# Rotary partners of queries and keys by a partition shuffle, with their squares on ScalarE

## The chip, the cores and the metric

One of the cores of a Trainium2 chip runs the whole program. The metric is the device time of one execution in microseconds. Five engines matter: TensorE (PE; its weight loads are PEld), VectorE (DVE), ScalarE (ACT), GpSimd (POOL) and SyncE (SP), which issues the loads of weights.

## What is computed

Two layers of a hybrid block (a convolution, a retention and a window attention branch on one input projection), and then one layer of another block. Sequence 512, width 1024, all in fp32. The change touches the attention branch of the two hybrid layers alone:

```python
def window_attention_branch(q, k, v, gate, q_norm_g, k_norm_g, sink, positions):
    q = rms_norm(q.reshape(B, S, ATTN_HEADS, HEAD_DIM), q_norm_g)      # 16 heads of 64
    k = rms_norm(k.reshape(B, S, ATTN_KV_HEADS, HEAD_DIM), k_norm_g)   # 4 heads of 64
    q = rotary(q, positions, ROPE_THETA, ROPE_DIM)                     # first 16 of each 64
    k = rotary(k, positions, ROPE_THETA, ROPE_DIM)
    ...
    s = jnp.where(valid, s, -1e30)                                     # window of 128 to each side
    m = jnp.maximum(jnp.max(s, axis=-1, keepdims=True), sink_l)
    p = jnp.exp(s - m)
    p = p / (jnp.sum(p, axis=-1, keepdims=True) + jnp.exp(sink_l - m))
    o = jnp.einsum('bhgnqj,bnjhd->bnqhgd', p, vwin)
    return o.reshape(B, S, ATTN_HEADS * HEAD_DIM) * jax.nn.silu(gate)

def rotary(x, positions, theta, rot_dim):
    x1, x2 = x[..., :half], x[..., half:rot_dim]                       # half is 8
    return concatenate([x1 * cos - x2 * sin, x2 * cos + x1 * sin, x[..., rot_dim:]])
```

## The kernel before

Activations lie transposed: a tile is 128 features (partitions) by 512 positions. A weight slab is 128x1024. SyncE loads it into one of two `raw` buffers; ScalarE rounds it to fp32r (`high`, L832, tile `whi`), GpSimd takes the rest (`low`, L275, `wlo`), each into one of four buffers. TensorE then makes each product as three fp32r matmuls, high by high, high by low, low by high (L330 to L332 in `gemm`, L521 to L523 in `rows`). Results stand in the four banks of `gem`; a bank is free when `evac` of it has counted up. The other PSUM tensor, `xp`, has four banks for everything that is not a slab product. Every engine has its program written out by hand, in order; they meet only at semaphores.

Keys and queries of the attention branch are ten tiles of two heads each, `NORMED[0..9]`: two of keys, eight of queries. For each tile n:
- VectorE squares it into the scratch `RT[0]` (`square`, L1600, signal `a_sq`)
- TensorE adds the squares over each 64 partitions: a product with the block matrix `blk64` into bank 0 of `xp` (`a_norm`, L484, signal `a_ssq`). This and the next are plain fp32 matmuls, which the chip runs as two passes
- ScalarE makes the inverse root by logarithm and exponential into `RS` (`a_inv`, L849 and L851, signal `a_rs`)
- VectorE multiplies by it (`a_normed`, L1606, signal `a_kn`)
- TensorE multiplies by a rotation matrix `rot` into bank 1 of `xp` (`a_turn`, L489, signal `a_rot`)
- VectorE rotates: tile times cosines into `RT[1]` (L1612), `xp` times sines into `RT[2]` (L1614), sum (L1616, signal `a_rope`). This is `a_rotated`

Tiles 0 to 5 go through this while TensorE makes the queries' first half and the last retention head's output product (`half`; its results are added to `yr` on VectorE, L1555). "The head" below is that stretch. Tiles 6 to 9 go through it in the attention stage: TensorE first makes slabs 0 to 3 (queries' second half, `rows(k, ...)`) and then goes through 24 steps t, three per pair of heads (p = t // 3). In step t it makes the scores of step t (`qk`, L544; from step 2 on it waits for `p_exp` of step t - 2's exponentials), transposes the probabilities of step t - 3 (`turn_p`, L562), multiplies step t - 4's with the values (`a_pv`, L578), and makes a part of gate slab 4 + p (`rows`) in between. ScalarE makes the exponentials of a step (`exps`, L1027), copies transposed probabilities to `PT`, and a tanh for the gate (L1047); VectorE makes the masked maxima (`maxes`, L1660 to L1666), the normaliser (`normalise`, L1673 and L1675, for the first step of a pair L1683 too) and the gate (L1689, which frees bank 3). GpSimd scales the probabilities of the other two steps (L284).

The scratch lies where other buffers live later: `RT[0]` and `RT[1]` in the first buffer of transposed probabilities `PT[0]`, `RT[2]` in the second, `PT[1]`. So the transposes of step 0 wait for all ten rotations (`a_rope`).

Of the kernel before, what the change touches and what calls it, by code (L numbers as in the profile page):

```python
# [26 lines left out]
PAD = TAPS // 2  # L27

# [41 lines left out]
def build(nc, ins, out, xsave):  # L70
# [5 lines left out]
    with ctx:  # L76
# [17 lines left out]
        rot = sb("rot", [P, P])  # L94
# [37 lines left out]
        RT = [U[:, a:a + T] for a in (U_C + 2 * T, U_C + 3 * T, U_SG + 2 * T)]  # L132
# [41 lines left out]
        def sem(name):  # L174
# [32 lines left out]
        a_sq, a_ssq, a_rs, a_kn, a_rot, a_rope = (sem(n) for n in (  # L207
            "a_sq", "a_ssq", "a_rs", "a_kn", "a_rot", "a_rope"))
# [105 lines left out]
        def _(pe):  # L314
# [70 lines left out]
            def layer(L):  # L385
# [6 lines left out]
                if L == 0:  # L392
                    pe.wait_ge(const_in, 16 * 6)
# [105 lines left out]
                for k in range(1, 4):  # L499
                    hslab(G + 2, k, u + 2)  # L500
                    if k > 1:
                        a_turn(k - 2)
                    a_norm(k - 1)
                for k in range(4):
                    half(G + 3, k, u + 3, (z_ready, L * 40 + 12 + PRIMED) if k == 0 else None)
                    a_turn(k + 2)
# [41 lines left out]
                def turn_p(t):  # L548
# [6 lines left out]
                    if t == 0:  # L555
                        pe.wait_ge(a_rope, L * 10 + 10)
# [27 lines left out]
                for k in range(1, 4):  # L584
# [3 lines left out]
                    a_turn(k + 5)  # L588
                    if k == 2:
                        qk(0)  # L590
                for t in range(1, 24):
# [7 lines left out]
                    if t == 2:  # L599
                        a_turn(9)  # L600
# [216 lines left out]
        def _(act):  # L817
# [4 lines left out]
            for n, (dst, name) in enumerate(((ident, "ident"), (blk64, "blk64"), (rot, "rot"), (amask, "amask"),  # L822
# [65 lines left out]
            def layer(L):  # L888
# [101 lines left out]
                read(0, QR[0], A.Copy)  # L990
                for v in range(2):
# [4 lines left out]
                for k in range(1, 4):  # L996
                    tick(G + 2, k)
                    read(k, QR[k], A.Copy)
                    a_inv(k - 1)
                high(G + 3, 3)  # L1000
                for k in range(3):
                    high(G + 3, k + 4)
                    a_inv(k + 3)

                act.wait_ge(z_ready, L * 40 + 16 + PRIMED)
                G, u = g0 + ATT[0], u0 + ATT[1]
                tick(G, 0)
                read(0, QR[4], A.Copy)

# [21 lines left out]
                for k in range(1, 4):  # L1031
# [5 lines left out]
                    read(k, QR[4 + k], A.Copy)  # L1037
                for t in range(1, 27):
# [294 lines left out]
        def _(dve):  # L1333
# [84 lines left out]
            def layer(L):  # L1418
# [29 lines left out]
                if L == 0:  # L1448
                    dve.wait_ge(const_in, 16 * 6)
# [142 lines left out]
                ua = u0 + ATT[1]  # L1592

                def square(n):
                    dve.drain()
                    if n >= 6:
# [648 lines left out]
```

## Time and profile before

| | |
|---|---|
| Median of 3 runs | 3121.58 us (3121.37 to 3121.99) |
| The profiled execution | 3118.49 us |
| Its span, first to last instruction | 3116.7 us |
| Mean granted TensorE clock | 0.995 of full |
| Busy: PE, DVE, ACT, POOL | 98%, 55%, 35%, 45% of the span |

A busy share is an average over very different stages. In a row of the timeline stand start, duration, engine, line, operation, the tiles written and read, and in brackets how long the engine had been idle and who ended that. Matmuls are pipelined: their durations overlap, and the step from one start to the next is what one costs.

### The profile page before, as it was taken

How to read it: one execution, taken by the hardware profiler on the slowest of the kernel's cores; microseconds unless marked ns; L12 is line 12 of the kernel's file. 1: busy time of each engine (PE TensorE's matmuls, PEld its weight loads, DVE VectorE, ACT ScalarE, POOL GpSimd, SP SyncE). 2: the span in 40 equal slices, each digit the busy share in tenths (PEclk: the TensorE clock that was granted, in tenths of full speed). 3: DMA queues.
4: the chain of work that ended last, by engine and by line, in shares of the span. 5: the costliest groups of instructions: out<-in, count | busy, mean ns of one | idle time of the engine just before them, and what ended most of it. 6: DMA issues, size and time to landing. Idle time of an engine off the chain costs nothing.

```text
span 3116.7 us, 40813 instructions
## 1 busy us (share of the span) xinstructions
PE 3050.8 (98%) x13780; PEld 2404.0 (77%) x13780; DVE 1706.2 (55%) x2577; ACT 1092.9 (35%) x1635; POOL 1398.9 (45%) x1030
## 2 busy tenths in 40 slices
PE   7999999999999999999999999999999999999997
PEld 5877777767888787777776788877888887788886
DVE  7974575675434597576566644267763253621214
ACT  3232332354332223233235524235554332422223
POOL 4433543445555443443344455443334444454443
PEclk9999999999999999999999999999999999999999
DMA  3221222212222321221221132221212322222222
GB/s 139 95 73 69 94 71 78 81 42 82 95 101 98 112 103 68 95 74 67 81 82 54 35 129 95 100 88 61 71 70 88 103 86 97 85 102 95 96 100 81
DMA packets 73408, 267.86 MB, mean 86 GB/s; under 512 B 8144, under 2 KB 9168, under 8 KB 72912
## 3 DMA queue, kind: packets, MB, share of 16 engines
q1 hardware_dynamic: 70560, 254.84, 23.6%
q10 hardware_dynamic: 2736, 11.53, 1.0%
q8 instruction: 70, 1.15, 0.1%
q14 instruction: 42, 0.34, 0.0%
HBM read 262.14 MB, written 4.19 MB: 85 GB/s over the span
## 4 chain that ended last, share of the span: by engine, by line
PE 83%; issue 7%; POOL 5%; DVE 3%; DVEq 1%; ACT 1%; ACTq 0%; POOLq 0%
PE gem L330 18%; PE gem L332 18%; PE gem L331 18%; POOL wlo L275 5%; PE xp L434 4%; PE gem L410 2%; PE gem L409 2%; PE gem L411 2%; PE xp L423 2%; PE gem L521 2%; PE gem L523 1%; PE gem L522 1%; PE gem L544 1%; PE xp L578 1%; PE gem L677 1%
## 5 line engine op out<-in xcount | busy, mean ns | idle before, releaser
L275 POOL TENSOR_TENSOR wlo<-raw,whi 128x512 fp32r<-128x512 f32 x956 | 1318.9, 1401 | 1641.3 <-ACT whi L832 1640.5
L330 PE MATMUL gem<-hhi,whi 128*128 128x512 f32 x2032 | 813.0, 400 | 0.0
L332 PE MATMUL gem<-hhi,wlo 128*128 128x512 f32 x2032 | 791.3, 389 | 0.0
L331 PE MATMUL gem<-hlo,whi 128*128 128x512 f32 x2032 | 790.7, 389 | 0.0
L832 ACT ACTIVATE whi<-raw 128x1024 fp32r<-128x1024 f32 x478 | 504.4, 1056 | 679.7 <-PE gem L332 488.6
L330 PEld LDWEIGHTS gem<-hhi,whi 128*128 128x128 f32 x2032 | 381.6, 188 | 90.3 <-issue 12.9
L331 PEld LDWEIGHTS gem<-hlo,whi 128*128 128x128 f32 x2032 | 381.7, 188 | 89.7 <-issue 12.2
L332 PEld LDWEIGHTS gem<-hhi,wlo 128*128 128x128 f32 x2032 | 381.4, 188 | 79.8
L330 PE MATMUL gem<-zhi,whi 128*128 128x512 f32 x960 | 378.6, 394 | 2.9 <-DVE zlo L1346 2.9
L332 PE MATMUL gem<-zhi,wlo 128*128 128x512 f32 x960 | 374.1, 390 | 0.0
L331 PE MATMUL gem<-zlo,whi 128*128 128x512 f32 x960 | 374.0, 390 | 0.0
L841 ACT ACTIVATE U<-gem 128x512 f32<-128x512 f32 x150 | 89.2, 597 | 507.6 <-PE gem L332 456.0
L330 PEld LDWEIGHTS gem<-zhi,whi 128*128 128x128 f32 x960 | 180.4, 188 | 43.2 <-DVE zlo L1346 3.5
L331 PEld LDWEIGHTS gem<-zlo,whi 128*128 128x128 f32 x960 | 180.5, 188 | 39.6 <-issue 2.4
L332 PEld LDWEIGHTS gem<-zhi,wlo 128*128 128x128 f32 x960 | 180.4, 188 | 37.8
L1474 DVE SCALAR_TENSOR_TENSOR xp<-cv,sm,xp 128x512 f32<-128x512 f32 x224 | 159.1, 752 | 17.2 <-issue 15.0
L1441 DVE SCALAR_TENSOR_TENSOR xp<-cv,vec,xp 128x512 f32<-128x512 f32 x224 | 159.0, 752 | 9.2
L841 ACT ACTIVATE U<-gem,vec 128x512 f32<-128x512 f32 x96 | 65.5, 684 | 252.8 <-PE gem L332 217.7
L2055 DVE TENSOR_TENSOR U<-gem,U 128x512 f32<-128x512 f32 x22 | 15.2, 691 | 185.5 <-PE gem L332 185.5
L1346 DVE TENSOR_TENSOR zlo<-U,zhi 128x512 f32 (+1 forms) x88 | 107.8, 1225 | 11.4 <-issue 0.8
L434 PE MATMUL xp<-U 128*128 128x512 f32 x256 | 112.5, 592 | 0.0
L677 PE MATMUL gem<-hhi,whi 128*128 128x512 f32 x256 | 107.4, 419 | 0.5 <-POOL wlo L275 0.5
(265 smaller groups left out, 3902.1 us busy)
## 6 DMA issues: line engine op xcount, KB each, us to landing
raw<-in_slabs SPq DMA_DIRECT2D x478, 512.0 KB, 3.2
U<-in_x SPq DMA_DIRECT2D x4, 512.0 KB, 7.5
U<-in_x ACTq DMA_DIRECT2D x1, 2048.0 KB, 8.2
xsave<-U ACTq DMA_DIRECT2D x1, 2048.0 KB, 6.3
U<-xsave ACTq DMA_DIRECT2D x1, 2048.0 KB, 8.3
out_y<-yr SPq DMA_DIRECT2D x8, 256.0 KB, 2.1
tab<-in_tab_ret ACTq DMA_DIRECT2D x2, 512.0 KB, 8.0
tab<-in_tab_att ACTq DMA_DIRECT2D x2, 512.0 KB, 3.6
```

The source lines that it names most:

```text
L275: part = pool.tensor_tensor(wlo[:, k % 4, c], raw[:, k % 2, c], whi[:, k % 4, c].bitcast(f32), O.subtract)
L330: pe.matmul(o, wh, hi, start=(n == 0), stop=False)
L331: pe.matmul(o, wh, lo, start=False, stop=False)
L332: mm = pe.matmul(o, wl, hi, start=False, stop=(n == len(terms) - 1))
L409: pe.matmul(o, hhi[:, k, c], wh, start=(k == 0), stop=False)
L434: mm = pe.matmul(xp[:, v % 2, :], VT[:, j, v * P:(v + 1) * P], ST[:, j, :], start=(j == 0), stop=(j == 3))
L677: pe.matmul(gem[:, k, :], wh, hhi[:, r, :], start=(r == 0), stop=False)
L832: act.activation(whi[:, k % 4, :], raw[:, k % 2, :], A.Copy).then_inc(hi_done, 1)
L841: act.activation(dst, gem[:, b, :], func, bias=bias, scale=scale).then_inc(evac[b], 1)
L1346: tt(lo, src, hi.bitcast(f32), O.subtract).then_inc(count, 1)
L1441: stt(acc if n < TAPS - 1 else TT[:, 0, :], v, w, acc, O.mult, O.add)
L1474: stt(acc if n < TAPS - 1 else TT[:, 0, :], v, w, acc, O.mult, O.add)
```

## The change

It computes the rotated partner on VectorE. A shuffle of the 32 partitions of each quadrant swaps rows 0 to 7 with rows 8 to 15 (`PARTNER`), and the sign that was in the matrix `rot` is now in the sine table. `rot`, its load, `a_turn` and the signal `a_rot` are gone. The squares are activations on ScalarE, right after it has read a tile's bank or, for tiles that are there already, after the inverse root of the tile before. `RT[1]` and `RT[2]` both lie in the second buffer `PT[1]`; so the transposes of step 0 wait only for the tenth inverse root, those of step 1 for the ten rotations, and the last rotation is made in step 3 instead of step 2. VectorE normalises step 0 ahead of the maxima of step 1 and makes a head tile's rotation ahead of the addition to `yr`.

```diff
+PARTNER = [r + 8 if r < 8 else r - 8 if r < 16 else r for r in range(32)]
...
-        RT = [U[:, a:a + T] for a in (U_C + 2 * T, U_C + 3 * T, U_SG + 2 * T)]
+        RT = [U[:, a:a + T] for a in (U_C + 2 * T, U_SG + 2 * T, U_SG + 3 * T)]
...
# TensorE
-                def a_turn(n):
-
-                    pe.wait_ge(a_kn, L * 10 + n + 1)
-                    pe.matmul(xp[:, 1, :], rot[:, :], NORMED[n], start=True, stop=True).then_inc(a_rot, 1)
...
                     if t == 0:
+                        pe.wait_ge(a_rs, L * 10 + 10)
+                    elif t == 1:
                         pe.wait_ge(a_rope, L * 10 + 10)
...
# ScalarE
                 def a_inv(n):
                     act.wait_ge(a_ssq, L * 10 + n + 1)
+                    if n:
+                        act.wait_ge(a_kn, L * 10 + n)
                     inv_sqrt(RS, xp[:, 0, :], 64, EPS, a_rs)
+
+                def a_square(n):
+
+                    act.activation(RT[0], NORMED[n], A.Square).then_inc(a_sq, 1)
...
                 read(0, QR[4], A.Copy)
+                act.drain()
+                a_square(6)
...
                     read(k, QR[4 + k], A.Copy)
+                    act.drain()
+                    a_square(k + 6)
...
# VectorE
                     tt(RT[1], x, tab[:, 0, :], O.mult)
-                    dve.wait_ge(a_rot, L * 10 + n + 1)
-                    tt(RT[2], xp[:, 1, :], tab[:, 1, :], O.mult)
+                    dve.stream_shuffle(RT[2], x, PARTNER)
+                    dve.drain()
+                    tt(RT[2], RT[2], tab[:, 1, :], O.mult)
...
                 maxes(0)
                 a_rotated(7)
                 a_normed(8)
-                square(9)
+                normalise(0)
+                maxes(1)
                 a_rotated(8)
-                maxes(1)
-                normalise(0)
                 a_normed(9)
                 for t in range(2, 24):
                     p, c = t // 3, t % 3
                     maxes(t)
                     normalise(t - 1)
-                    if t == 2:
+                    if t == 3:
                         a_rotated(9)
...
# tables
-            cos[h + r:h + r + 8], sin[h + r:h + r + 8] = ca, sa
+            cos[h + r:h + r + 8], sin[h + r:h + r + 8] = ca, sa if r else -sa
```

On TensorE, in the head, after the second slab of queries, this piece of the difference (a minus is a row of before that is gone) stands six times per layer, with small variations:

```order
 L331 MATMUL gem<-hlo,whi 128x512
 L332 MATMUL gem<-hhi,wlo 128x512
-L489 MATMUL xp<-U,rot 128x512
 L484 MATMUL xp<-U,blk 128x512
 L330 MATMUL gem<-hhi,whi 128x512
```

The rotation between the slab and the sum over squares is gone; the slab's last matmul and the sum now follow each other.

On ScalarE, at attention slabs 0 and 1, before (`U<-gem` is the read of a bank, `whi<-raw` the conversion of a weight slab, the two rows with `U` after it an inverse root):

```order
L841 ACTIVATE U<-gem 128x512
L832 ACTIVATE whi<-raw 128x1024
L849 ACTIVATE U<-xp,sm 128x512
L851 ACTIVATE U<-U 128x512
L841 ACTIVATE U<-gem 128x512
L832 ACTIVATE whi<-raw 128x1024
```

and in the change (L984 is the square):

```order
L832 ACTIVATE U<-gem 128x512
L984 ACTIVATE U<-U 128x512
L823 ACTIVATE whi<-raw 128x1024
L840 ACTIVATE U<-xp,sm 128x512
L842 ACTIVATE U<-U 128x512
L832 ACTIVATE U<-gem 128x512
L984 ACTIVATE U<-U 128x512
```

A square now stands between the read of a tile and the next weight conversion.

On VectorE, in step 2 of the attention stage, before: the end of the maxima, the normaliser of step 1, the last rotation (L1612, L1614, L1616), the gate, and the maxima of step 3.

```order
L1664 SCALAR_TENSOR_TENSOR sm<-sm 128x2
L1666 TENSOR_TENSOR sm<-sm 128x2
L1673 TENSOR_TENSOR sm<-sm 128x2
L1675 RECIPROCAL sm<-sm 128x2
L1612 TENSOR_TENSOR U<-U,tab 128x512
L1614 TENSOR_TENSOR U<-xp,tab 128x512
L1616 TENSOR_TENSOR U<-U 128x512
L1689 SCALAR_TENSOR_TENSOR U<-U,gem 128x512
L1660 ISA gem,sm<-gem,amask 128x256
```

In the change, in step 3: the end of the maxima of step 3, the normaliser of step 2, the last rotation with its shuffle, and the first of the maxima of step 4.

```order
L1651 SCALAR_TENSOR_TENSOR sm<-sm 128x4
L1653 TENSOR_TENSOR sm<-sm 128x4
L1660 TENSOR_TENSOR sm<-sm 128x2
L1662 RECIPROCAL sm<-sm 128x2
L1608 TENSOR_TENSOR U<-U,tab 128x512
L1609 STREAM_SHUFFLE U<-U 128x512
L1611 TENSOR_TENSOR U<-U,tab 128x512
L1613 TENSOR_TENSOR U<-U 128x512
L1647 ISA gem,sm<-gem,amask 128x384
```

The rotation moved behind a gate and one more step of maxima, and no operand of it is in PSUM any more.

## Rows read from the trace of the kernel before

**Rows 1.** The page, first part: busy us (share of the span) xinstructions.

```profile
PE 3050.8 (98%) x13780; PEld 2404.0 (77%) x13780; DVE 1706.2 (55%) x2577; ACT 1092.9 (35%) x1635; POOL 1398.9 (45%) x1030
```

**Rows 2.** Waits of PE in the span: waited for: us in total, times, longest.

```profile
PE xp L562 <- DVE U L1616: 3.6, 2, 1.8
```

**Rows 3.** Line 489, the rotation product: duration ns min/median/max, first and last start.

```profile
L489 PE MATMUL xp<-U,rot x40: 591/592/592, 565.4 to 1675.8; 128*128 128x512 f32 x40
```

**Rows 4.** Timeline of PE in the head.

```profile
572.63 1.02 PE L489 MATMUL xp<-U,rot 128*128 128x512 f32 x2
573.48 1.02 PE L484 MATMUL xp<-U,blk 128*128 128x512 f32 x2
```

**Rows 5.** Lines 1600, 1612, 1614 and an activation of that width (x40 | us, mean ns).

```profile
L1600 DVE TENSOR_TENSOR U<-U x20: 691/692/694, 554.5 to 1667.3; 128x512 f32<-128x512 f32 x20
...
L1612 DVE TENSOR_TENSOR U<-U,tab x20: 691/1602/1675, 563.2 to 1677.0; 128x512 f32<-128x512 f32 x20
...
L1614 DVE TENSOR_TENSOR U<-xp,tab x20: 676/681/693, 566.5 to 1677.6; 128x512 f32<-128x512 f32 x20
...
L857 ACT ACTIVATE U<-U 128x512 f32<-128x512 f32 x40 | 24.6, 629 | 53.6 <-DVE U L1798 29.1 <-DVE U L1357 10.6 <-DVE U L1352 8.2
```

**Rows 6.** Timeline of ACT in the attention stage.

```profile
607.97 0.60 ACT L841 ACTIVATE U<-gem 128x512 f32<-128x512 f32 x1 [5.20 <-PE gem L523]
...
630.47 0.60 ACT L841 ACTIVATE U<-gem 128x512 f32<-128x512 f32 x1
...
637.63 1.28 ACT L1044 ACT_TABLE_LOAD   x1
...
641.09 0.59 ACT L1047 ACTIVATE U<-gem 128x512 f32<-128x512 f32 x1
```

**Rows 7.** Timeline of PE in the attention stage.

```profile
610.49 1.02 PE L484 MATMUL xp<-U,blk 128*128 128x512 f32 x2
...
626.22 1.02 PE L484 MATMUL xp<-U,blk 128*128 128x512 f32 x2
...
631.63 0.50 PE L521 MATMUL gem<-hhi,whi 128*128 128x512 f32 x1
...
635.17 1.02 PE L484 MATMUL xp<-U,blk 128*128 128x512 f32 x2
...
640.40 0.45 PE L544 MATMUL gem<-U 64*128 64x256 f32 x1 [0.24 <-ACT sm L1029]
...
643.35 1.06 PE L562 MATMUL xp<-ident,U 128*128 128x128 f32 x8 [1.82 <-DVE U L1616]
...
648.07 0.82 PE L562 MATMUL xp<-ident,U 128*128 128x128 f32 x6
```

**Rows 8.** Timeline of DVE there: tile 8's rotation, then maxima and normalisers.

```profile
631.88 0.69 DVE L1612 TENSOR_TENSOR U<-U,tab 128x512 f32<-128x512 f32 x1
632.49 0.68 DVE L1614 TENSOR_TENSOR U<-xp,tab 128x512 f32<-128x512 f32 x1
633.25 0.69 DVE L1616 TENSOR_TENSOR U<-U 128x512 f32<-128x512 f32 x1
...
639.76 0.16 DVE L1666 TENSOR_TENSOR sm<-sm 128x2 f32<-128x2 f32 x1
...
643.72 0.43 DVE L1660 CUSTOM_DVE_ANT_0 gem<-gem,amask 128x256 f32<-128x256 f32 x1
...
645.74 0.48 DVE L1673 TENSOR_TENSOR sm<-sm 128x2 f32<-128x2 f32 x1
```

**Rows 9.** Windows, 554 to 602 us: us, then busy (x) of PE, PEld, DVE, ACT, POOL.

```profile
554.00:602.00 48.00, 48.00 (x192) 35.69 (x191) 28.80 (x35) 17.48 (x25) 21.17 (x14) 1.00 0.24 85
```

**Rows 10.** Timeline of POOL in the attention stage, then of DVE under its work.

```profile
644.40 4.90 POOL L284 TENSOR_SCALAR U<-U,sm 128x384 f32<-128x384 f32 x4
...
651.71 2.53 POOL L275 TENSOR_TENSOR wlo<-raw,whi 128x512 fp32r<-128x512 f32 x2 [2.40 <-ACT whi L832]
...
653.06 1.20 DVE L1664 SCALAR_TENSOR_TENSOR sm<-sm 128x2 f32<-128x2 f32 x1
```

More of the change, by code:

```diff
@@ L205, in build @@
         osq, ossq, ovar, orstd = (sem(n) for n in ("osq", "ossq", "ovar", "orstd"))
-        a_sq, a_ssq, a_rs, a_kn, a_rot, a_rope = (sem(n) for n in (
-            "a_sq", "a_ssq", "a_rs", "a_kn", "a_rot", "a_rope"))
+        a_sq, a_ssq, a_rs, a_kn, a_rope = (sem(n) for n in ("a_sq", "a_ssq", "a_rs", "a_kn", "a_rope"))
         s_done, m_ready, p_exp, r_ready, p_ready0, p_ready1 = (sem(n) for n in (
@@ L821, in _ @@
             act.dma_start(vec[:, :], ins["vecs"][0]).then_inc(vec_in, 16)
-            for n, (dst, name) in enumerate(((ident, "ident"), (blk64, "blk64"), (rot, "rot"), (amask, "amask"),
+            for n, (dst, name) in enumerate(((ident, "ident"), (blk64, "blk64"), (amask, "amask"),
                                              (dist, "dist"), (vec2, "vec2"))):
@@ L998, in layer @@
                     read(k, QR[k], A.Copy)
+                    if k == 1:
+                        act.wait_ge(z_ready, L * 40 + 16 + PRIMED)
                     a_inv(k - 1)
+                    a_square(k)
                 high(G + 3, 3)
@@ L1003, in layer @@
                     a_inv(k + 3)
-                act.wait_ge(z_ready, L * 40 + 16 + PRIMED)
+                    if k < 2:
+                        a_square(k + 4)
                 G, u = g0 + ATT[0], u0 + ATT[1]
@@ L1590, in layer @@
                 gated(3)
[L1592 to L1596, printed above, removed]
-                        dve.wait_ge(evac[n - 6], ua + 1 + PRIMED)
-                    elif n >= 2:
-                        dve.wait_ge(evac[n - 2], u + 3 + PRIMED)
-                    tt(RT[0], NORMED[n], NORMED[n], O.mult).then_inc(a_sq, 1)
                 def a_normed(n):
@@ L1612, in a_rotated @@
                     tt(RT[1], x, tab[:, 0, :], O.mult)
[L1613 to L1614 removed]
+                    dve.stream_shuffle(RT[2], x, PARTNER)
+                    dve.drain()
+                    tt(RT[2], RT[2], tab[:, 1, :], O.mult)
                     dve.drain()
                     tt(x, RT[1], RT[2], O.add).then_inc(a_rope, 1)
[L1618 to L1619 removed]
                 dve.wait_ge(tab_in, L * 32 + 32)
                 apart(dve)
[L1622 to L1624 removed]
                 for n in range(2):
+                    a_normed(n)
                     a_rotated(n)
[L1627 to L1628 removed]
+                a_normed(2)
                 for k in range(4):
+                    a_rotated(k + 2)
                     add_out(G + 3, u + 3, (k,))
[L1631 removed]
                     if k < 3:
                         a_normed(k + 3)
[L1634 to L1635 removed]
                 ts(NSK, vec[:, C_SINK:C_SINK + 16], -1.0, None, O.mult)
[L1637 to L1643 removed]
+                u = u0 + ATT[1]
+                a_normed(6)
+                a_rotated(6)
+                a_normed(7)
                 def per_head(tile, p, k):
@@ L2205 @@
     cos, sin = np.ones((P, T), f), np.zeros((P, T), f)
-    rot = np.zeros((P, P), f)
     for h in (0, 64):
         for r in (0, 8):
-            cos[h + r:h + r + 8], sin[h + r:h + r + 8] = ca, sa
-        for r in range(8):
-            rot[h + 8 + r, h + r] = -1.0
-            rot[h + r, h + 8 + r] = 1.0
+            cos[h + r:h + r + 8], sin[h + r:h + r + 8] = ca, sa if r else -sa
     part, col = np.arange(P)[:, None], np.arange(P)[None, :]
@@ L2231 @@
         "gm_b": np.broadcast_to(a["gm_b_s_2"][0][None], (P, NT, P)),
-        "ident": np.eye(P, dtype=f), "blk64": (part // 64 == col // 64).astype(f), "rot": rot, "amask": amask,
+        "ident": np.eye(P, dtype=f), "blk64": (part // 64 == col // 64).astype(f), "amask": amask,
         "dist": (np.arange(896)[None, :] - part - 384).astype(np.int16),
```

29 lines of the change are left out of this document (3 added, 26 removed).

## The prediction

> **What bounds the kernel now.** I read the page's first part, then who TensorE waited for, then the order of time around the two attention stages. TensorE is busy 98% of the span [rows 1] at a granted clock of 0.995 of full, and nearly everything that the chain of waits passes through is its matmuls. So an instruction taken off TensorE is worth its own time, as long as nothing else comes due in its place. In the attention stage TensorE waits once per layer: 1.8 us for the last rotation's final addition on VectorE, 3.6 us in both layers [rows 2]. All clock times below are those of the first layer; the second repeats them about 1036 us later.
>
> **Taken off TensorE: 20 products with the rotation matrix.** There are ten per layer, each of two passes, so 40 records [rows 3]. The passes overlap, so the duration of a record (0.59 us) is not the price. The price is the step from start to start: 572.63 to 573.48, 0.85 us [rows 4]. All twenty come to 17.1 us.
>
> **Moved or exchanged on the other engines.** (a) Ten squares per layer leave VectorE (0.69 us each) and go to ScalarE, where a 512-wide activation takes 0.63 us [rows 5]. ScalarE now makes them right after it has read the bank. For the seventh tile that read runs 607.97 to 608.57 [rows 6]; with the square it is done at 609.3, just where VectorE was done, and TensorE's sum over it starts at 610.49 [rows 7]. The other squares in that stage have the same distance, the earlier ones more, since ScalarE then idles for most of a slab. Behind each square stands the conversion of the next slab's weights (`high`), 0.65 us later and needed slabs later: cost nothing. The new wait for `a_kn` asks for a normalisation that VectorE did one tile earlier: nothing. (b) Each rotation gains a shuffle and keeps three two-operand instructions. No shuffle is in this trace. The nearest rows by width and type are the 512-wide square at 0.69 us and the product with the table at 0.68 us [rows 5]; I take 0.69 plus 0.08 for the drain behind it (the drain between 632.49 + 0.68 and 633.25 [rows 8]), 0.77 us. The low end is 0.35 us, half of it, if a copy-like instruction ran at double rate; the high end is 1.68 us, the longest 512-wide row of this group [rows 5]. (c) The sine product used to read PSUM and always took 0.68 us; its sibling with two SBUF operands takes 0.69 us when GpSimd is idle and 1.6 to 1.68 us when GpSimd makes low parts [rows 5]. So up to 1 us per rotation is added where GpSimd runs.
>
> The Trainium skill, "VectorE: DVE Perf Modes", section "The perf-mode tier table", gives the shuffle one rate only, about 2400 ns for 2048 elements; less 1536 elements at one per 0.96 GHz cycle that is an estimate of 0.8 us for 512. With it the sum below would be 0.2 us smaller. No run here shows it yet.
>
> **Ahead of the attention slabs: six of ten rotations per layer.** From 554 to 602 us VectorE is busy 28.80 of 48.00 us [rows 9]. Six rotations fall there: six shuffles add 4.6 us, stretched sine products at most 6 us, six squares leave with 4.2 us: 35.2 us in the 42.9 us that remain. VectorE's deadlines there (freeing a bank pair) are about a slab away, so the gain stands whole: 6 x 0.85 = 5.1 us per layer.
>
> **In the attention stage** the removed steps are four, and here other chains are close behind. I follow how far TensorE is ahead of its old times, not counting the 5.1.
> - Rotations 6, 7, 8: 2.56 us ahead by the fourth bank. But slab 4 writes bank 3, which ScalarE must have read first. From the ninth sum (626.22) ScalarE needs until 631.07 for inverse root, exponentials and that read; TensorE came there at 631.63 [rows 6, 7]. The margin was 0.56 us, the ninth rotation's 0.85 is more: a new wait of about 0.35 us. Ahead: 2.2 us.
> - Rotation 9: from the tenth sum (635.17) ScalarE makes an inverse root, loads a table (1.28 us from 637.63), and exponentials of step 1; the scores of step 3 wait for these and start at 640.40, 5.23 us after the sum, already with 0.24 us of idleness [rows 6, 7]. ScalarE's chain starts from the sum and is not shortened, so the 0.85 us becomes wait. Still 2.2 us ahead: scores 3 at 638.2.
> - The old wait for the last rotation: scores 3 ended 1.13 us after their start (643.35 less 1.82 of wait is 641.53 [rows 7]), so the first transposes now start at 639.35, unhindered. The gate behind them needs ScalarE's tanh (641.09 + 0.59, less 2.2, is 639.5 [rows 6]) and 0.69 us on VectorE: ready at 640.2, as the transposes end. Until then TensorE is 4.0 us ahead.
> - The last rotation now stands behind maxima 3 and normalisation 2. Maxima 3 run from 640.2 and take 2.0 us (643.72 to 645.74), the normaliser's two small instructions with their drains some 0.6 [rows 8]: the rotation starts at about 642.9. Its length: 2.06 us (631.88 to 633.25 + 0.69 [rows 8]) plus 0.77 for the shuffle, 2.83 us if GpSimd leaves it alone. GpSimd scales probabilities then; under that work one small instruction took 0.48 us (at 645.74) where the like take 0.16 (at 639.76) [rows 8], others lost nothing. I take 0.35 for the three two-operand instructions together: 3.2 us, done at 646.1. The transposes of step 1, which must not overwrite the scratch, used to start at 648.07 [rows 7]; TensorE alone, 3.9 us ahead, would reach them at 644.2. So the old wait of 1.8 us comes back as one of 1.9 us one step later. Ahead for good: 2.0 us. Step 4's maxima are late too, but TensorE asks for their exponentials only at the scores of step 6.
>
> **The sum.** 5.1 + 2.0 = 7.1 us per layer, 14.2 us in both. Everything behind the stage follows TensorE and moves up. The profiled execution took 3118.49 us (span 3116.7) and would take 3104.3. The median of the runs is 3121.58, 3.1 us above it, which the edit doesn't touch: 3107.4 us. The ends of the shuffle (0.35, 1.68) and of the shared access (none, 1.0) move the last rotation by -0.7 to +1.6 us per layer: 3106.0 to 3110.6. The rotations before it have room even then: maxima 2 ended at 639.92, and their exponentials could not begin before the tanh was over at 641.68 [rows 6, 8], 1.7 us to spare, and both move alike with the tenth sum.
>
> **Rivals.**
> 1. *The whole price comes back*: no new waits, and the old ones gone: 17.1 + 3.6 = 20.7 us, 3100.9. It needs the last rotation at or before 644.2, that is 1.3 us long after 642.9, against three instructions that sum to 2.06 us even without the shuffle. Against it too stand the 0.56 us and the 5.23 us above. 8%, near 3102 at best if my waits are half as long.
> 2. *GpSimd's access shuts VectorE out for whole instructions.* At 653.06 a VectorE instruction on two columns took 1.20 us: it stood until the second half of a low part, begun at 651.71 and 2.53 us long, was over. Under the probabilities (four in 4.90 us from 644.40) [rows 10] the small rows were hardly held, but no full-width one lies there. If each of the last rotation's three were held until the instruction in progress ends (1.2 us at most, some 0.6, 0.4 and 1.1), it lasts 4.9 us, to 647.8, and TensorE is ahead by 0.3 us: 5.4 per layer, 10.8 in all, 3110.8. 17%.
> 3. *The other side, slower than before: the shuffle makes VectorE the bound.* Place: each of the ten rotations. In the head VectorE has 7.7 us to spare per layer by the count above, in the attention stage the 1.7 us just named, at the last rotation none. An excess of x per shuffle over 0.69 costs about 6x - 7.7 us in the head and 3x - 1.7 in the stage; the two eat the gain of 7.1 from x = 1.8, a shuffle of 2.5 us. At 3.5 us they would cost 15.9 and leave 8.8 us of loss per layer: 3139. The slowest full-width row is 1.68 us, and that is queueing. 3%.
> 4. *Nothing to be measured*: another bound just behind, such as the path of the weights, gives the gain back in both layers; 3119. In these stages the trace has TensorE waiting for nothing but the 1.8 and the 0.24 us. 4%.
>
> Rival 2 is what the Trainium skill states in "SBUF — State Buffer", section "SBUF: two separate sides": a VectorE instruction with two SBUF inputs and a GpSimd instruction take a shared port pair in turns, each for its whole length. The rows under the low parts agree (1.6 against 0.69 us); the small ones under the probabilities rather don't.
>
> **How the numbers follow.** Forecast (gain of 11.0 to 15.6 us) 68%, rival 1 8%, rival 2 17%, rival 3 3%, rival 4 4%. 0.2% of the time, about what a measurement of this kernel can tell from no change, is 6.2 us; forecast and rivals 1 and 2 all gain more. Faster 0.93, same 0.04, slower 0.03. The range takes in the forecast and rival 2 with the ends above and stops short of rivals 1, 3 and 4, which leave 15% outside: 3102.5 to 3111.5.
>
> **What would show it.** Right: twenty products gone and start-to-start spacing elsewhere unchanged; TensorE 5.1 us early at the first attention slab; new idleness of about 0.4 us ahead of slab 4, 1.1 us ahead of scores 3, and 1.9 us ahead of the transposes of step 1, released by the rotation's last addition; shuffles of 0.7 us; the attention stages' head with no TensorE wait. Wrong: shuffles well off 0.7 us; a wait in the head for a bank or for `a_sq`; the transposes of step 1 released by GpSimd's probabilities; or a gain that is not the same in both layers.

## The result, and the profile after

| | before | change |
|---|---|---|
| Median of 5 runs each, us | 3121.61 (3121.37 to 3122.18) | 3103.95 (3103.47 to 3106.0) |
| Profiled execution, us | 3118.49 | 3103.47 |
| Its span, us | 3116.7 | 3101.7 |
| Mean granted TensorE clock | 0.995 | 0.995 |

The ratio is 0.9944 (95%: 0.993 to 0.9959): faster by 17.7 us, where 14.2 were forecast. The two traces differ by 15.0 us. The first part of the page of the change, to be laid beside [rows 1]:

```profile
PE 3034.5 (98%) x13740; PEld 2396.6 (77%) x13740; DVE 1710.6 (55%) x2597; ACT 1104.2 (36%) x1655; POOL 1393.3 (45%) x1030
```

TensorE has 40 records fewer, VectorE 20 more (20 squares gone, 20 shuffles and the loads of their masks added), ScalarE 20 more. The shares hardly move, and they tell little; who TensorE waited for tells more. The waits of PE in the change (waited for: us in total, times, longest), which answer to [rows 2]:

```profile
PE xp L556 <- issue: 3.4, 2, 1.7
...
PE gem L536 <- ACT sm L1033: 2.2, 2, 1.1
...
PE gem L513 <- ACT U L832: 0.7, 2, 0.4
```

The old wait of 1.8 us per layer is gone. In its place stand three, one each per layer: 1.7 us ahead of a pair of transposes (L556, before L562), 1.1 us ahead of scores (L536, 0.24 us before), and 0.4 us ahead of a gate slab (L513) for ScalarE's read of the bank. Where they stand shows the timeline of PE in the attention stage, to be read against [rows 7]:

```profile
604.89 1.02 PE L484 MATMUL xp<-U,blk 128*128 128x512 f32 x2
...
623.86 0.47 PE L513 MATMUL gem<-hhi,whi 128*128 128x512 f32 x1 [0.37 <-ACT U L832]
...
632.59 0.45 PE L536 MATMUL gem<-U 64*128 64x256 f32 x1 [1.10 <-ACT sm L1033]
...
633.65 1.09 PE L556 MATMUL xp<-ident,U 128*128 128x128 f32 x8
...
640.54 0.85 PE L556 MATMUL xp<-ident,U 128*128 128x128 f32 x6 [1.75 <-issue]
```

TensorE is 5.60 us early at the first sum of the stage (610.49 before); 7.81 us at scores 3 (640.40); 9.70 us at the transposes of step 0 (643.35), which wait for nothing now; and 7.53 us at those of step 1 (648.07), where the old wait stands again, one step later. The profile puts this last wait down to "issue", no engine. What it was shows the timeline of DVE (VectorE), which answers to [rows 8]:

```profile
637.29 0.70 DVE L1608 TENSOR_TENSOR U<-U,tab 128x512 f32<-128x512 f32 x1
...
637.93 0.75 DVE L1609 STREAM_SHUFFLE U<-U 128x512 f32<-128x512 f32 x1
638.76 0.69 DVE L1611 TENSOR_TENSOR U<-U,tab 128x512 f32<-128x512 f32 x1
639.52 0.92 DVE L1613 TENSOR_TENSOR U<-U 128x512 f32<-128x512 f32 x1
```

The rotation of the tenth tile ends at 640.44, the transposes start at 640.54. It is 3.15 us long, and its sum took 0.92 instead of 0.69 us: GpSimd was scaling probabilities, and its four instructions took longer than before as well (4.90 us in [rows 10]):

```profile
636.05 5.74 POOL L284 TENSOR_SCALAR U<-U,sm 128x384 f32<-128x384 f32 x4
```

Rows by line, which answer to [rows 5]: the rotation's four instructions (L1608 stands for L1612 of before, L1611 for L1614), and the square, now on ScalarE (duration ns min/median/max):

```profile
L1608 DVE TENSOR_TENSOR U<-U,tab x20: 691/694/704, 562.1 to 1666.2; 128x512 f32<-128x512 f32 x20
...
L1609 DVE STREAM_SHUFFLE U<-U x20: 720/738/756, 562.7 to 1666.8; 128x512 f32<-128x512 f32 x20
...
L1611 DVE TENSOR_TENSOR U<-U,tab x20: 691/693/1089, 563.5 to 1667.6; 128x512 f32<-128x512 f32 x20
...
L1613 DVE TENSOR_TENSOR U<-U x20: 692/693/1623, 565.0 to 1668.4; 128x512 f32<-128x512 f32 x20
...
L984 ACT ACTIVATE U<-U x20: 614/620/635, 553.0 to 1652.7; 128x512 f32<-128x512 f32 x20
```

**The ruler.** Medians of one kernel differ between sets of runs by 1 us. The experiments need less, so I measure a stretch inside the traces: from the transposes of the values ahead of the queries to the last transposes of the attention stage, in the first layer. In both kernels it holds all that the change touches. Before, by PE's timeline:

```profile
552.73 1.03 PE L496 MATMUL xp<-ident,U 128*128 128x128 f32 x8
...
754.42 0.82 PE L562 MATMUL xp<-ident,U 128*128 128x128 f32 x6
```

and in the change:

```profile
552.33 1.03 PE L491 MATMUL xp<-ident,U 128*128 128x128 f32 x8
...
746.95 0.82 PE L556 MATMUL xp<-ident,U 128*128 128x128 f32 x6
```

That is 201.69 and 194.62 us: 7.07 us, 7.1 having been forecast. In the second layer it is 201.62 (1589.01 to 1790.63) and 194.48 (1581.31 to 1775.79): 7.14 us. The 15.0 us of the span are these 14.21, 0.40 ahead of the first stretch, 0.23 between them and 0.16 behind the second. "The stretch" below is that of the first layer. It rests on one trace of each kernel. The medians of most experiments (3104.2 to 3104.9 us for e2, e5, e6 and e7) can't be told from the change's own (3103.95 and 3104.7), so what they show is shown by the stretches of their two layers.

### The profile page after: what moved, and what is told of

It is laid out like the page before. It is cut to its first block, busy times and chain, and to the rows that moved or that the text cites. A ratio compares the mean times of both kernels' runs of the same rounds, so it can differ in the third digit from the quotient of the medians.

```text
span 3101.7 us, 40798 instructions
## 1 busy us (share of the span) xinstructions
PE 3034.5 (98%) x13740; PEld 2396.6 (77%) x13740; DVE 1710.6 (55%) x2597; ACT 1104.2 (36%) x1655; POOL 1393.3 (45%) x1030
## 4 chain that ended last, share of the span: by engine, by line
PE 83%; issue 7%; POOL 5%; DVE 3%; ACT 1%; DVEq 1%; DMA 0%; POOLq 0%; ACTq 0%; SPq 0%
PE gem L330 19%; PE gem L332 18%; PE gem L331 18%; POOL wlo L275 5%; PE xp L434 4%; PE gem L409 2%; PE gem L410 2%; PE gem L411 2%; PE xp L423 2%; PE gem L513 2%; PE gem L515 1%; PE gem L514 1%; PE xp L572 1%; PE gem L536 1%; PE gem L668 1%
```

## Experiments

**The change once more** (r1_change), as the yardstick for the traces.

> The change itself, run again beside the experiments and beside the kernel before. Theory A (everything that the trace shows: 17.1 us of products less 2 x 0.37, 2 x 1.10 and 2 x 1.7 us of new waits, plus 2 x 1.8 and 2 x 0.24 of old ones, plus 0.44 us at the program's start = 15.3 us): its executions at an equal clock are 14.8 to 15.3 us shorter than those of before, and a larger ratio comes from executions in which TensorE ran slow for some microseconds. Rival B (there is a gain of about 2.5 us that the trace does not show): the unprofiled pairs stay at 17.7 us.

Measured: 3104.7 us (3103.95 to 3105.63), before 3121.18 (3118.78 to 3121.88), ratio 0.9949 (0.9932 to 0.9966). The stretch is 194.56 us, the three waits 1.7, 1.1 and 0.4 us. So the stretch of the change repeats within 0.1 us (that of v2 below only within 0.5), where the spans, 3101.7 and 3103.8, differ by 2.1. Where 1.6 of the 2.1 us arise shows the window 14 to 40 us (us, busy (x) of PE, PEld, DVE, ACT, POOL, then the granted clock), first this run, then the profiled one above:

```profile
14.00:40.00 26.00, 20.84 (x62) 14.45 (x63) 18.79 (x25) 5.29 (x6) 8.75 (x6) 0.80 0.23 83
```

```profile
14.00:40.00 26.00, 20.23 (x69) 14.39 (x70) 18.52 (x25) 5.48 (x6) 8.75 (x6) 1.00 0.24 83
```

Here TensorE comes out of some 14 us without work. In one execution part of the first products ran at the lower level of its clock (1.2 GHz, a granted clock of 0.50 from 22 to 31 us: 16 matmuls of 0.63 us between 20 and 40 us, where the other has 5), and the transposes at 552.33 stand at 553.96. That is a difference of executions, not of kernels.

Neither theory is borne out as it stands. The medians differ by 16.5 us, not 17.7 (rival B). At an equal listed mean clock the medians over all sets differ by 16.0 us (0.995), 15.5 (0.994) and 16.1 (0.993), a little more than the 14.8 to 15.3 of theory A; the clock is listed to three places only, and the change has 2 to 5 executions at each.

**Are the 14 us TensorE's own time?** (e1_dead_products) The change, with twenty products back on TensorE where the rotations had stood. Nothing waits for them or reads them.

```diff
+                def dead_turn():
+
+                    pe.matmul(xp[:, 1, :], rot[:, :], cv[:, 0, 0:T], start=True, stop=True)
...
                 for k in range(4):
                     half(G + 3, k, u + 3, (z_ready, L * 40 + 12 + PRIMED) if k == 0 else None)
+                    dead_turn()
...
                     rows(k, 4, 8)
+                    dead_turn()
...
+                    if t == 2:
+                        dead_turn()
```

> The change with twenty dead products put back on TensorE in the places of the rotation products (matrix rot by a finished tile of the convolution, result read by nobody) and the matrix's load put back. Squares on ScalarE, shuffles and order stay as in the change. Theory A (the gain is TensorE's time and nothing else): the span goes back to before's 3116.7 us, or 0.3 us per layer above it, 3117.3, since the last rotation now ends later; the waits ahead of slab 4 (0.37) vanishes and that ahead of scores 3 falls from 1.10 to about 0.24 us; ahead of the transposes of step 1 about 2 us stay. The first TensorE instruction is 0.44 us later than in the change. Rival C (moving the squares and the rotations' order gains by itself): 3 us or more below before, 3113 or less.

Measured: 3121.28 us (3118.63 to 3122.27, 10 runs), ratio 1.0002 (0.9992 to 1.0011), span 3116.8: theory A, and not rival C. The stretch is 552.65 to 754.64, 201.99 us, 0.3 more than before; in the second layer 201.88. PE's timeline:

```profile
640.32 0.45 PE L544 MATMUL gem<-U 64*128 64x256 f32 x1 [0.24 <-ACT sm L1044]
...
648.24 0.85 PE L564 MATMUL xp<-ident,U 128*128 128x128 f32 x6 [1.73 <-issue]
```

The whole gain is gone with the twenty products alone. The matrix holds zeros here, but a product with it takes as long as before: 621.27 us to the next start at 622.22, where before had 621.35 to 622.30. The wait ahead of scores 3 is back at the 0.24 us of before, slab 4 waits for nothing, and the last rotation is still waited for, 1.73 us. So the squares on ScalarE, the new order and the deferral together save nothing against the kernel before; what is saved is 17.1 us of matmuls, less the waits that take their place.

**Squares back on VectorE** (e5_squares_back).

```diff
-                def a_square(n):
-
-                    act.activation(RT[0], NORMED[n], A.Square).then_inc(a_sq, 1)
...
+                def square(n):
+                    dve.drain()
...
+                    tt(RT[0], NORMED[n], NORMED[n], O.mult).then_inc(a_sq, 1)
```

> The change with all ten squares back on VectorE, each right after the normalisation of the tile before (the tenth after tile 8's). Theory A (the squares lie off the path on either engine): span within 0.5 us of 3101.7; the tenth's normalisation is some 0.5 us later and maxima 2 still end before the exponentials ask for them. Rival G (with shuffles and squares VectorE is too late): TensorE waits for sums or for step 2's exponentials, 1 us or more per layer, 3104 or more.

Measured: 3104.36 us (3103.96 to 3106.26), ratio 0.9948 (0.9931 to 0.9965), stretch 194.57 and in the second layer 194.46, the waits unchanged. That is theory A by the stretch and not rival G; the span of its trace, 3102.8, lies 1.1 us above the change's, outside the stretches. Moving the squares is worth nothing in either direction, which closes the question that e1 left.

**The last rotation without its shuffle** (e2_last_shuffle_out). The tenth tile's partner is left out; its sine product takes the tile itself.

```diff
-                    dve.stream_shuffle(RT[2], x, PARTNER)
-                    dve.drain()
-                    tt(RT[2], RT[2], tab[:, 1, :], O.mult)
+                    if n < 9:
+                        dve.stream_shuffle(RT[2], x, PARTNER)
+                        dve.drain()
+                        tt(RT[2], RT[2], tab[:, 1, :], O.mult)
+                    else:
+                        tt(RT[2], x, tab[:, 1, :], O.mult)
```

> The change without the shuffle of the tenth tile: its partner product takes the unshuffled tile (left out: the tenth tile's rotary partner, so its rotation is not the reference's). Theory A (of ten rotations only the last is on the path): the transposes of step 1 wait 0.8 us less per layer, 1.6 us in all: span 3100.1. Rival D (they wait for GpSimd's scaled probabilities, which end at about the same time): no change, 3101.7.

Measured: 3104.92 us (3101.72 to 3105.97), ratio 0.9949 (0.9933 to 0.9966), span 3102.1; stretch 193.86, 0.76 less than the change, and 193.72 in the second layer, 0.76 less again, which is theory A's 0.8. The median hides that, the stretch doesn't. PE's timeline names another releaser now:

```profile
639.69 0.85 PE L556 MATMUL xp<-ident,U 128*128 128x128 f32 x6 [0.97 <-POOL U L284]
```

That name is wrong, as the rotation's sum in DVE's timeline and the second of GpSimd's four scalings in POOL's show:

```profile
638.90 0.69 DVE L1616 TENSOR_TENSOR U<-U 128x512 f32<-128x512 f32 x1
```

```profile
637.19 1.75 POOL L284 TENSOR_SCALAR U<-U,sm 128x384 f32<-128x384 f32 x1
```

These transposes need the first two scalings, one for each head, and those were done at 638.94. The rotation ended at 639.59, 0.10 us ahead of the transposes, just as in the change (640.44 and 640.54). So the 0.97 us are still a wait for the rotation, and rival D fails: one shuffle of 0.74 us on the path is 0.76 us of time. TensorE was ready at 638.72; without the rotation it would have waited only some 0.2 to 0.3 us for GpSimd, and v1 below shows 0.31.

**The nine others without theirs** (e3_nine_shuffles_out): the same edit the other way round, `if n == 9` for the branch with the shuffle.

> The change without the shuffles of tiles 0 to 8, only the tenth's kept (left out: the rotary partners of nine tiles). Theory A: eighteen shuffles of 0.74 us, 13.3 us of VectorE time in all, are worth 0.0 to 0.4 us of span: 3101.3 to 3101.7. Rival E (VectorE's load in the head sets part of the pace): 1 us or more.

Measured: 3106.66 us (3104.41 to 3107.7), ratio 0.9954 (0.9937 to 0.997), stretch 195.06, 0.44 **more** than the change; in the second layer 194.51, where the change has 194.48. Eighteen shuffles off the path bring nothing: theory A, but for the small loss, which neither theory had. Where the first layer lost its 0.44 us shows DVE's timeline:

```profile
639.05 0.70 DVE L1608 TENSOR_TENSOR U<-U,tab 128x512 f32<-128x512 f32 x1
...
639.69 0.74 DVE L1610 STREAM_SHUFFLE U<-U 128x512 f32<-128x512 f32 x1
640.87 1.02 DVE L1612 TENSOR_TENSOR U<-U,tab 128x512 f32<-128x512 f32 x1 [0.44 <-issue]
641.96 0.69 DVE L1616 TENSOR_TENSOR U<-U 128x512 f32<-128x512 f32 x1
```

The last rotation, untouched, was caught otherwise by GpSimd's work (four scalings in 5.95 us from 637.81). VectorE stood 0.44 us idle ahead of the sine product, where the drain alone takes 0.08, and started it 0.08 us after a scaling had ended (639.04 to 640.79); the product then took 1.02 us. Over its usual course that is 0.69 us of holding in all. In both layers of the change it was 0.23, in the first layer of v2 0.66. So the hold differs from meeting to meeting, by where in GpSimd's instructions the rotation falls.

**The last rotation in step 2, where it was** (e4_last_in_step2).

```diff
-                    if t == 3:
+                    if t == 2:
                         a_rotated(9)
```

> The change with the last rotation back in step 2, ahead of the gate; the scratch stays in the second buffer. Theory A (the deferral only moves the wait): no wait ahead of the transposes of step 1, but TensorE waits about 1.8 us per layer for the gate, which frees bank 3, ahead of slab 5; span within 0.5 us of the change's 3101.7. Rival F (the deferral itself gains): the rotation ahead of the gate costs 2 us or more in all, 3103.7 or more.

Measured: 3110.25 us (3107.67 to 3112.58, 6 runs), ratio 0.9964 (0.9952 to 0.9977); stretch 553.63 to 752.05, 198.42 us, 3.8 more than the change; in the second layer (1586.43 to 1783.62) 2.7 more. Theory A, that the deferral only moves a wait, is refuted; rival F, 2 us or more in all, holds. DVE's timeline:

```profile
635.71 0.93 DVE L1611 TENSOR_TENSOR U<-U,tab 128x512 f32<-128x512 f32 x1
636.71 1.60 DVE L1613 TENSOR_TENSOR U<-U 128x512 f32<-128x512 f32 x1
638.23 0.67 DVE L1676 SCALAR_TENSOR_TENSOR U<-U,gem 128x512 f32<-128x512 f32 x1
```

PE's, from the gate's release on:

```profile
639.05 0.76 PE L513 MATMUL gem<-hhi,whi 128*128 128x512 f32 x1 [3.02 <-DVE U L1676]
...
640.47 0.63 PE L513 MATMUL gem<-hhi,whi 128*128 128x512 f32 x1
...
641.88 1.65 PE L536 MATMUL gem<-U 64*128 64x384 f32 x4
```

and the window around it (columns as above; the clock is the last number but two):

```profile
639.00:644.80 5.80, 5.75 (x13) 3.47 (x14) 3.09 (x16) 2.03 (x9) 4.11 (x4) 0.50 0.26 87
```

Two things add up. The rotation stands ahead of the gate (L1676), under a low part of GpSimd (634.75 to 637.76), and its last sum takes 1.60 us; TensorE waits for the gate 3.02 us, not for transposes 1.8. And after these 3.0 us without a matmul the granted clock is 0.50 for 5.8 us, the level of 1.2 GHz: the four score products take 1.65 us where they take 0.92 in the change. The deferral is worth nothing against the kernel before (e1), but this change needs it: 3.8 and 2.7 us in the two layers. The wait of 3.02 us stands in both; less the one ahead of the transposes that it replaces (1.75 and 1.66 us) it explains 1.3 and 1.4 us. The rest, 2.5 and 1.35 us, is left for the slower matmuls, of which the second layer has a shorter piece (a granted clock of 0.52 from 1673 to 1676 us).

**The last rotation in step 2, but behind the gate** (e7_last_behind_gate). There it delays no gate, and is done 2.5 us earlier than in step 3.

```diff
-                    if t == 3:
-                        a_rotated(9)
...
+                    if t == 2:
+                        a_rotated(9)
```

> The change with the last rotation in step 2 behind the gate, ahead of the maxima of step 3. Theory A (what cost 3.0 us in the kernel with it ahead of the gate was bank 3; behind the gate nothing asks for VectorE until the scores of step 5): no wait ahead of slab 5, the transposes of step 1 wait for GpSimd at most (0 to 1 us) and scores 5 for maxima 3 by 0 to 0.5 us; 1.5 to 3.4 us less than the change. Rival K (the rotation, now under GpSimd's low parts, is held to 4 us, and maxima 3 come too late for scores 5): TensorE waits 1.5 us or more per layer at scores 5, no gain over the change.

Measured: 3104.39 us (3101.38 to 3106.04), ratio 0.9948 (0.9932 to 0.9965), span 3099.6; stretch 193.67, 0.95 less than the change, in the second layer 193.64, 0.84 less: 1.8 us in all, within theory A's 1.5 to 3.4. The median shows nothing of it. The transposes of step 1 wait 0.7 us, here for GpSimd indeed: the rotation's sum was done at 637.94, the second scaling at 639.28. The stretch is as short as in e2, where work was left out, with all of the work done.

**Scratch of its own** (v1_scratch_apart). The cosine product and the partner lie in two tiles that nothing else needs until the gated heads of steps 6 and 9 (`ZT`), so the transposes of step 1 wait for no rotation.

```diff
-        RT = [U[:, a:a + T] for a in (U_C + 2 * T, U_SG + 2 * T, U_SG + 3 * T)]
+        RT = [U[:, a:a + T] for a in (U_C + 2 * T, U_VT + 3 * T, U_VF + T)]
...
-                    elif t == 1:
-                        pe.wait_ge(a_rope, L * 10 + 10)
```

> The change with the rotation's scratch in two tiles that are free until steps 6 and 9 (the gated heads' ZT), so no transposes wait for a rotation; order unchanged. Theory A (the last new wait is that for the scratch): the wait of 1.7 us ahead of the transposes of step 1 goes, except what GpSimd's probabilities leave of it (0 to 0.5 us): span 3098.3 to 3099.3. Rival H (the next chain, maxima 4 late behind the rotation, takes its place): scores 6 wait, 3100.5 or more.

Measured: 3101.61 us (3100.82 to 3104.18), ratio 0.994 (0.9923 to 0.9956), stretch 193.17, 1.45 less, in the second layer 193.06, 1.42 less. PE's timeline:

```profile
640.46 0.88 PE L554 MATMUL xp<-ident,U 128*128 128x128 f32 x6 [0.31 <-POOL U L284]
```

The whole wait was 1.75; 0.31 us of GpSimd's stay, as theory A had it, and scores 6 don't wait (rival H). Its span was missed, though: 3099.9 at a mean clock of 0.994, not 3098.3 to 3099.3. The rotation still ends after the transposes have begun; what made them wait for it was the shared buffer.

**Exponentials ahead of the inverse root** (e6_exps_first_alone: the change with this edit; v2_exps_first: v1 with it). ScalarE makes the exponentials of step 1 first, then the tenth inverse root and the load of its table, so that scores 3 find them done.

```diff
                     if t == 1:
+                        exps(1)
                         a_inv(9)
                         act.preload_act_table_set("exp_and_others")
...
-                    if t < 24:
+                    if 1 < t < 24:
                         exps(t)
```

> The change with only the exponentials of step 1 moved ahead of the tenth inverse root and the table load; the scratch stays in the second buffer. Theory A (the two waits are links of one chain: gate, maxima 3 and last rotation follow ScalarE's step 2, so they move up too): the wait ahead of scores 3 goes (1.10 us per layer) and that ahead of the transposes of step 1 stays at about 1.7 us: 2.2 us less in all, a span of 3099.5 at the clock of the first profile of the change. Rival J (the last rotation does not move up): the wait there grows to 2.8 us and the span stays.

> The kernel with the scratch apart, and the exponentials of step 1 ahead of the tenth inverse root and of the table load, while ScalarE was idle. Theory A (scores 3 wait for that chain and nothing else stands close behind): the wait of 1.10 us ahead of scores 3 goes too, 2.2 us in all: span 3096.1 to 3097.5. Rival I: the gate, whose tanh still needs the table load, stops TensorE 0.5 to 1 us later at slab 5, and half or more of the 2.2 us comes back: 3097.5 to 3099.

Measured: e6 3104.24 us (3100.67 to 3105.27), ratio 0.9942 (0.9926 to 0.9959), stretch 193.40, 1.22 less than the change (1.20 in the second layer), the wait ahead of scores 3 gone and the one ahead of the transposes still 1.7. That is theory A in the trace; the median is no lower than the change's. v2 3099.46 us (3098.38 to 3100.55), ratio 0.9932 (0.9915 to 0.9949), span 3096.6 (theory A), stretch 191.45: 3.17 less. In the second layer it is 191.84, 2.64 less, and in the repeat below 2.66, which is just 1.22 and 1.45 together. In the first layer a single wait is left in its attention stage, that of slab 4 (the second has besides 0.22 us for GpSimd ahead of the transposes of step 1):

```profile
623.68 0.47 PE L513 MATMUL gem<-hhi,whi 128*128 128x512 f32 x1 [0.37 <-ACT U L830]
```

**The bank's read first as well** (v3_read_first): v2 with the read of bank 3 ahead of `exps(0)` on ScalarE, and maxima 1 ahead of the first normaliser on VectorE.

```diff
-                    if k == 3:
-                        exps(0)
                     act.wait_ge(slab_done, G * 4 + (k + 1) + PRIMED)
                     read(k, QR[4 + k], A.Copy)
+                    if k == 3:
+                        exps(0)
```

> The kernel with scratch apart and exponentials first, and besides ScalarE reads bank 3 ahead of the exponentials of step 0, and VectorE makes maxima 1 ahead of normaliser 0. Theory A: the wait of 0.37 us ahead of slab 4 goes and nothing takes its place: 0.7 us less than that kernel. Rival L: the exponentials of step 0 end 1.9 us later, the later chain slips, and TensorE waits 0.4 us or more elsewhere.

Measured: 3101.64 us (3099.7 to 3102.41), ratio 0.9937 (0.9921 to 0.9954), stretch 192.09. The wait for slab 4 is gone and another is there, for the gate, 1.0 us in the first layer; in the second, by PE's timeline:

```profile
1661.89 0.77 PE L513 MATMUL gem<-hhi,whi 128*128 128x512 f32 x1 [2.23 <-DVE U L1675]
1662.46 0.63 PE L514 MATMUL gem<-hlo,whi 128*128 128x512 f32 x1
```

Again the lower clock follows the idleness. The stretch of the second layer is 194.71 us, 2.9 more than v2's. So rival L holds: doing away with 0.37 us cost more than it gave. The run makes two edits at once, so which of them costs it stays open. v2 stands.

**v2 once more** (v2_again), since it is the best of them.

> The kernel with scratch apart and exponentials first, again, beside the one that reads bank 3 first. Theory A: 3098.4 to 3101 us, 20.5 to 22.5 us below before, waits of TensorE in the attention stage of 0.37 us per layer and no others.

Measured: 3098.98 us (3096.87 to 3100.65), before 3121.5 (3119.76 to 3122.12); ratio 0.9927 (0.9911 to 0.9944), stretch 191.96 and in the second layer 191.85. Besides the wait of 0.37 us there is one for GpSimd ahead of the transposes of step 1, 0.28 and 0.20 us, which the expectation didn't have. By its two runs v2 is 22 us faster than the kernel before and some 5 us faster than the change.

## Why the prediction was right, and where it was off

**The price of a product.** Right. Ten of them put back (e1) make the stretch 7.37 us longer (201.99 less 194.62), while the waits ahead of slab 4 and of scores 3 shrink by 0.37 and 0.86 us: 8.60 us for ten, 0.86 each, where the start-to-start step gave 0.85. The records' own durations, 2 x 0.59 us, would have made it 1.18.

**The head.** 5.1 us per layer forecast. At the first sum of the attention stage TensorE is 5.60 us early, 0.40 of it from ahead of the stretch: 5.2. No wait for a bank or for `a_sq` arose. The count on VectorE was cautious: 30.65 us busy of 43, not 35.2 of 42.9, by the window that answers to [rows 9]:

```profile
554.00:597.00 43.00, 43.00 (x180) 33.38 (x179) 30.65 (x41) 19.62 (x30) 19.14 (x14) 1.00 0.28 91
```

The step that failed there: "up to 1 us per rotation is added where GpSimd runs", taken as an addition to the sine product. In [rows 5] the cosine product had a median of 1602 ns; now it is 694. Without the product on TensorE between them the instructions fall elsewhere in GpSimd's low parts, and what is held is the sine product (up to 1.09 us), the sum (up to 1.62) and the normalisation behind them (1.87 us at 580.34). Over 0.69 us each, the full-width instructions on SBUF of the head's six tiles are held 7.0 us in all before (554 to 606 us) and 7.1 in the change (554 to 597 us). Holding is passed on, not added.

**The attention stage.** Each wait came where it was forecast: ahead of slab 4, 0.37 us (0.35); ahead of scores 3, 1.10 (1.1); none at the old place; ahead of the transposes of step 1, 1.75 and 1.66 us (1.9). The last rotation was forecast to start at 642.9 less the 5.1 us of the head, 637.8, less the 0.4 of the start 637.4; it started at 637.29 and was 3.15 us long (3.2). The sum of 7.1 us per layer measured 7.07 and 7.14. So close a hit is in part luck. By the prediction's own subtraction the wait ahead of slab 4 is 0.85 less 0.56, 0.29 us, and not the 0.35 that it went on with (0.37 came), and in the last rotation a shuffle 0.06 us dearer than forecast stands against a hold 0.12 us shorter.

**The shuffle.** 0.77 us forecast from start to start, with the drain. It takes 0.74 us and the next instruction starts 0.83 us after it (637.93 to 638.76). The Trainium skill, "VectorE: DVE Perf Modes", section "The perf-mode tier table", by the estimate of 0.8 us that the prediction made of it, is 0.06 us above the duration, about as far as my square was below it (0.69); the trace agrees with its single rate, and neither end (0.35, 1.68) was near.

**GpSimd against VectorE (rival 2).** The mechanism is there, its price was not. The last rotation was to be held 0.35 us by the forecast and 2.1 by the rival (4.9 less 2.83); it was held 0.23 in the change, 0.69 in a layer of e3. GpSimd's own scalings took 5.74 us instead of 4.90, so both engines lose. The Trainium skill, "SBUF — State Buffer", section "SBUF: two separate sides", has the two take turns for whole instructions; holds below the 1.2 us of one scaling, different with each meeting, and the delay on both sides agree with it. What the rival had wrong was to let all three instructions be held, for 2.1 us together, where one was. No run takes GpSimd's work away: that it is GpSimd that holds VectorE is read from which instructions lie beside each other.

**The other side (rival 3).** Far off: a shuffle of 0.74 us, not 2.5. Still, a loss of 3.8 and 2.7 us in the two layers lay one line away (e4), and I had it in no rival: not the shuffle's length but the place of the last rotation, ahead of the gate.

**The whole time.** 3107.4 us was forecast, 3.4 us too much. 0.8 us of it is the difference of the traces (15.0 for 14.2): 0.40 us ahead of the first stretch, 0.39 behind and between. The step that failed there is that nothing but the two layers' attention was counted. The load of `rot` is issued on ScalarE's queue ahead of its first activation, and takes half a microsecond there. Before (timeline of ACT at the start):

```profile
2.52 0.51 ACTq L824 DMA_DIRECT2D rot<-in_rot  x1
...
5.38 1.28 ACT L845 ACT_TABLE_LOAD   x1 [5.38 <-issue]
```

The change has no such row, and its table load starts at 4.94. I can't call this shown: with `rot` it started at 5.38 and 5.30, in kernels without it anywhere from 4.70 to 5.29. The other 2.7 us are the step from the profiled execution to the median, "3.1 us above it, which the edit doesn't touch". The step that failed there is this one: before, the median lies 3.1 us above the profiled execution; in the change it lies 0.5 above. Executions of one kernel differ by how long TensorE stays at its lower clock (before, over the sets that list it: a mean clock of 0.995 gives 3118.5 to 3121.1 us, 0.993 gives 3121.2 to 3122.1; the change: 3103.5 to 3104.1, and 3105.1 to 3105.6). The five executions of before in the first comparison all lie at 3121.4 us or above, among the slower ones; of the five of the change three have 0.995. The profiled execution of before, 3118.49 us, is the lowest of its kernel in any set, as is that of the change, 3103.47. At an equal mean clock the kernels differ by 15.5 to 16.1 us (see r1_change). So the edit is worth 15 us by the traces and up to 16 by the medians at equal clock, and of the 17.7 us of the first comparison some 2 to 3 belong to how the executions fell. Why that clock falls out otherwise, and where the 1 us between the traces and those medians lies, stays open.

## What to carry to other kernels

On a path that one engine fills, an instruction taken off it is worth its start-to-start step; then walk the order and ask at each place which chain is next, since each of them takes its part back (here 20.7 us offered, 14.2 kept in the two stretches). Where a deferred piece of work makes a wait, ask which buffer causes it before moving the work: scratch of its own (v1) and the exponentials of one step moved (v2) gave back 2.6 to 3.2 us per layer, where a whole shuffle taken off the path gave 0.76. Read the releaser of a wait from the other engine's timeline before believing its name (e2). And a wait of 3 us on TensorE cost more than 3 us here (e4): it was paid again in matmuls at the lower clock.

## What the runs showed of the hardware

- After 3.02 us without a matmul TensorE ran 5.8 us at a granted clock of 0.50, in the midst of a stage that is otherwise at full clock (e4, first layer); after 2.23 us some 3.4 us at 0.52 (v3, second layer). After waits of 2.19 us (e3, first layer), 1.75 and 1.10 us (the change) it didn't: 1.00 in the windows behind them.
- A partition shuffle of 128x512 fp32 costs 0.74 us, and the load of its mask 14 ns. GpSimd never held it: 718 to 764 ns over all shuffles of all runs, though the last one lies under a scaling. Each of the rotation's other three instructions is held in some run (the cosine product to 1.6 us before and in e5, the sine product to 1.09 and the sum to 1.62 in the change).
- A VectorE instruction held by GpSimd shows the hold in its duration or, in e3, as 0.44 us of idleness put down to "issue".
- A wait of TensorE for VectorE can be put down to "issue" (1.75 us to 640.54 in the change, the rotation's sum ending at 640.44) or to GpSimd (0.97 us to 639.69 in e2, the sum ending at 639.59): the releaser must then be read from the other engine's timeline.
